# An eleventh 2 MB expert-weight buffer in place of the residual rows; one buffer each for gathered and turned token rows; silu written in the place of h

## The chip, the cores and the metric

One Trainium2 chip; the kernel runs on one core of it. Engines are named as in the profile: PE (TensorE, matmul), PEld (its weight loads), DVE (VectorE), ACT (ScalarE), POOL (GpSimd), SP (SyncE, which here only issues transfers). The metric is the device time of one execution in microseconds (us), the median of the runs shown. The kernel before: 911.71 us, median of 3 runs (910.99 to 911.99).

## What is computed

The reference is one inference step of a one-layer encoder on 512 prompt rows and 32 sample rows of width 1024, 544 rows in all. Two mixers (a state-space branch and a pooling branch) are gated, merged, projected and added to the input. The result, x2, goes through a mixture of experts, and that stage is the one which the change touches:

```python
xn = _rmsnorm(x, g).reshape(b * l, dm)
...                                   # 4 groups of 8 experts; each row picks a group, then 2 experts in it
for e in range(N_EXPERTS):            # 32
    h = jax.nn.silu(xn @ w_gate[e]) * (xn @ w_up[e])
    y = y + combine[:, e:e + 1] * (h @ w_down[e]).astype(jnp.float32)
return x + y.reshape(b, l, dm).astype(x.dtype)
```

A last rmsnorm with `g_final` follows. `w_gate[e]` and `w_up[e]` are 1024 x 512, `w_down[e]` is 512 x 1024, all float32, so each is 2 MB (2.097 million bytes), and 32 experts need 96 such loads, 201 MB.

## The kernel before, in words

Everything of the core's SBUF is one tensor, `arena`, laid out by hand with the offsets `O_...`; so nearly every operand is called `arena` in the profile. All PSUM is one tensor, `ps`. The kernel is written per engine, in program order, with semaphores; there is no scheduler.

**Up to the experts.** The two mixers take the first 312 us. The output projection then makes x2 row block by row block (`out_part`, blocks of 128 rows, `OUT_ORDER`), DVE adds the residual into `x_tok` (the residual rows, 5 blocks of 1024 words at `O_XTOK`), POOL stores x2 to DRAM (`x2_rows`, L542), and router arithmetic assigns to each expert up to 64 row slots (`TILE`). Two experts make a pair: 128 slots, 16 pairs (`NP`). When all row numbers are known (`rows_ready`), the experts begin.

**The ring.** Expert weights go to a ring of 10 buffers of 2 MB (`RING`, `NS = 10`). Load l is kind l % 3 (gate, up, down) of expert l // 3, into buffer l % NS. All loads are issued by SP, in order (L390, with L419 and L423 for the last expert, whose loads are cut in pieces). Loads 0 to 6 are issued once the mixers' areas are free, load 7 after nine of ten output halves, loads 8 and 9 after the tenth. Load l from NS on waits in `freed(l)` for the last reader of load l - NS: `gu_done` (gate and up matmuls of that expert) or `down_done` (its down matmuls).

**One expert on PE** (loop at L1667, e = 0 to 32): gate and up matmuls of expert e (`gate_up`, L1637, 32 records of 128x512), after an odd e the turn of the next pair's gathered rows (`turn_x`, L1627, 8 transposes), the down matmuls of expert e - 1 (`down`, L1652, 16), then the turn of the gate and up results of e (`turn_gate_up`, L1644, 4).

**Round about it.** POOL gathers the rows of pair j from `x2_rows` into `xg[j % 2]` (L545, an indirect transfer), at first pairs 0 and 1 at once, then each gather when the turn of the pair two before it has emptied the buffer; it also scatters each expert's result to `y_parts` (L562). DVE copies the turned rows out of PSUM, times the norm's weight, into `xg_t[j % 2]` (`x_out`, L1268). ACT copies gate and up results to `gu_rows` (L748), and after their turn writes `silu[e % 2]` (L753); DVE multiplies into `h[e % 2]` (`hidden`, L1296), which `down` reads. `result` (L1300) copies the down result to `y_sb`.

**The end.** After the last weight load SP fetches x2 back (L427, L430) into ring buffers 6 and 7; after the last scatter it fetches `y_parts` (L445); PE sums (L1712), ACT and DVE norm with `g_b` (the row `g_final`, copied to all partitions, which ACT fetched to `O_GB` before the experts), and SP stores.

Between the last expert and the sums a branch handles experts with more than 64 rows (`overflow`, `more`); it is skipped for these inputs.

## Time and profile before

| | |
|---|---|
| runs shown | 910.99, 911.71, 911.99 us (median 911.71) |
| the profiled execution: its own time | 908.8 us |
| its span (first to last instruction) | 907.2 us |
| mean granted TensorE clock | 0.95 |
| PE busy | 800.0 us (88%) |
| DVE, ACT, POOL busy | 263.9, 120.0, 128.1 us (29%, 13%, 14%) |
| moved by DMA | 251.58 MB, mean 277 GB/s |
| expert stage (first gate matmul to last down matmul) | 406.99 to 875.4 us |

The profiled execution's own time is 1.6 us over its span and 2.9 us below the median of the runs. Busy shares are averages over stages that differ: before 312 us PE is nearly always busy and the DMA engines mostly are not; in the expert stage it is the other way round. So each part of the change is to be read in the stage in which it lies. Times in the rows are us from the span's start, "idle before" is the engine's own idle time ahead of the instruction with what ended it, and the transfers' "us to landing" is from the issue to the completion.

### The profile page before, as it was taken

How to read it: one execution, taken by the hardware profiler on the slowest of the kernel's cores; microseconds unless marked ns; L12 is line 12 of the kernel's file. 1: busy time of each engine (PE TensorE's matmuls, PEld its weight loads, DVE VectorE, ACT ScalarE, POOL GpSimd, SP SyncE). 2: the span in 40 equal slices, each digit the busy share in tenths (PEclk: the TensorE clock that was granted, in tenths of full speed). 3: DMA queues.
4: the chain of work that ended last, by engine and by line, in shares of the span. 5: the costliest groups of instructions: out<-in, count | busy, mean ns of one | idle time of the engine just before them, and what ended most of it. 6: DMA issues, size and time to landing. Idle time of an engine off the chain costs nothing.

```text
span 907.2 us, 9594 instructions
## 1 busy us (share of the span) xinstructions
PE 800.0 (88%) x3838; PEld 454.2 (50%) x3839; DVE 263.9 (29%) x745; ACT 120.0 (13%) x230; POOL 128.1 (14%) x224
## 2 busy tenths in 40 slices
PE   2999999999999899949998788788789877977986
PEld 2788888878888655543333233233223323323332
DVE  3799856510011245552111111011011101110115
ACT  3210021120100042420000000000000000000012
POOL 3000004870033300010110100010010101000000
PEclk9999999999999999959999999899899889989999
DMA  9520221426200294366999999999999999999946
GB/s 305 140 94 4 90 105 29 117 93 219 74 19 1 72 424 207 116 260 219 420 428 425 427 427 426 426 428 427 428 425 426 429 426 426 425 428 429 408 170 252
DMA packets 42671, 251.58 MB, mean 277 GB/s; under 512 B 13173, under 2 KB 14025, under 8 KB 29922
## 3 DMA queue, kind: packets, MB, share of 16 engines
q1 hardware_dynamic: 35292, 236.97, 64.1%
q0 software_dynamic: 6672, 12.86, 4.1%
q10 hardware_dynamic: 662, 1.13, 0.4%
q8 instruction: 31, 0.51, 0.2%
q14 instruction: 14, 0.11, 0.0%
HBM read 245.33 MB, written 13.46 MB: 285 GB/s over the span
## 4 chain that ended last, share of the span: by engine, by line
PE 64%; DMA 31%; DVE 2%; issue 1%; ACTq 1%; ACT 0%; SPq 0%; DVEq 0%; POOLq 0%
DMA arena<-in_w_exp_up 29%; PE ps L1385 26%; PE ps L1637 14%; PE ps L1531 6%; PE ps L1652 6%; PE ps L1712 2%; PE ps L1627 1%; PE ps L1470 1%; PE ps L1465 1%; PE ps L1519 1%; PE ps L1553 1%; DVE arena L845 1%; DMA arena<-in_cache_pool 1%; PE ps L1644 1%; ACTq L604 1%
## 5 line engine op out<-in xcount | busy, mean ns | idle before, releaser
L1637 PE MATMUL ps<-arena 128*64 128x512 f32 x1024 | 253.3, 652 | 64.1 <-DMA arena<-in_w_exp_up 63.0
L1385 PE MATMUL ps<-arena 128*128 128x272 f32 x1024 | 239.0, 395 | 0.0
L1385 PEld LDWEIGHTS ps<-arena 128*128 128x128 f32 x1024 | 195.2, 191 | 40.2
L1637 PEld LDWEIGHTS ps<-arena 128*64 128x64 f32 x1024 | 85.6, 150 | 209.1 <-issue 206.6
L1652 PE MATMUL ps<-arena 128*64 128x512 f32 x512 | 116.4, 595 | 1.3 <-DVE arena L1296 1.3
L1300 DVE TENSOR_SCALAR arena<-ps,arena 128x512 f32<-128x512 f32 x32 | 24.0, 751 | 208.3 <-PE ps L1652 208.3
L798 DVE TENSOR_TENSOR arena<-arena 128x256 f32<-128x256 f32 (+10 forms) x223 | 75.5, 339 | 11.4 <-ACT arena L705 3.9
L1268 DVE TENSOR_TENSOR arena<-ps,arena 128x1024 f32<-128x1024 f32 x16 | 19.6, 1225 | 186.3 <-PE ps L1627 186.3
L1652 PEld LDWEIGHTS ps<-arena 128*64 128x64 f32 x512 | 37.5, 137 | 65.1 <-issue 61.8
L562 POOL DMA_INDIRECT y_parts<-arena x32 | 31.9, 997 | 261.9 <-DVE arena L1300 261.9
L748 ACT ACTIVATE arena<-ps,arena 128x512 f32<-128x512 f32 x32 | 22.0, 687 | 315.1 <-PE ps L1637 315.1
L1531 PE MATMUL ps<-arena 128*128 128x512 f32 x128 | 59.6, 603 | 0.0
L545 POOL DMA_INDIRECT arena<-x_rows,arena x16 | 16.6, 1036 | 179.9 <-PE ps L1627 168.0
L1531 PEld LDWEIGHTS ps<-arena 128*128 128x128 f32 x128 | 22.7, 190 | 21.7 <-issue 21.5
L1127 DVE TENSOR_TENSOR arena<-ps,arena 128x544 f32<-128x544 f32 x8 | 5.8, 724 | 88.7 <-PE ps L1385 88.7
L1644 PEld LDWEIGHTS ps<-arena 128*128 128x128 f32 x128 | 17.9, 209 | 26.9 <-issue 25.1
L648 ACT ACTIVATE arena<-ps 128x544 f32<-128x544 f32 x20 | 12.5, 625 | 135.1 <-PE ps L1385 135.1
L753 ACT ACTIVATE arena<-ps 128x256 f32<-128x256 f32 x32 | 12.3, 384 | 125.8 <-PE ps L1644 125.8
L1368 PE MATMUL ps<-arena 128*128 128x128 f32 (+1 forms) x40 | 8.9, 399 | 18.2 <-DVE arena L845 18.2
L1644 PE MATMUL ps<-arena 128*128 128x128 f32 x128 | 23.9, 310 | 0.9 <-ACT arena L748 0.9
L1712 PE MATMUL ps<-arena 128*128 128x512 f32 x48 | 22.6, 633 | 2.3 <-issue 2.3
L1627 PEld LDWEIGHTS ps<-arena 128*128 128x128 f32 x128 | 16.1, 195 | 14.9 <-issue 12.2
(222 smaller groups left out, 484.5 us busy)
## 6 DMA issues: line engine op xcount, KB each, us to landing
arena<-in_w_exp_gate SPq DMA_DIRECT2D x31, 2048.0 KB, 28.0
arena<-in_w_exp_up SPq DMA_DIRECT2D x31, 2048.0 KB, 32.2
arena<-in_w_exp_down SPq DMA_DIRECT2D x31, 2048.0 KB, 37.6
arena<-in_w_in SPq DMA_DIRECT2D x6, 2048.0 KB, 9.3
arena<-in_x_prompt SPq DMA_DIRECT2D x8, 512.0 KB, 6.4
arena<-in_w_out SPq DMA_DIRECT2D x2, 2048.0 KB, 11.0
arena<-y_parts SPq DMA_DIRECT2D x4, 1024.0 KB, 8.0
arena<-in_w_glu_a SPq DMA_DIRECT2D x1, 2048.0 KB, 10.4
```

The lines of the kernel that those rows point to most:

```text
L562: pool.indirect_dma_start(out=y_parts, out_offset=bass.IndirectOffsetOnAxis(ap=y_row[:, e:e + 1], axis=0), in_=y_sb[e % 2], in_offset=None ...
L748: act.activation(gu_rows[par], ps[:, 2 + par, :], ACT.Copy, scale=scale).then_inc(gu_copied, 1)
L798: step(dve.tensor_tensor(out_, x0, x1, op))
L1268: dve.tensor_tensor(xg_t[par][:, :, 0:t], src[:, :, 0:t], g_x.unsqueeze(2).to_broadcast((P, KD, t)), ALU.mult).then_inc(xt_ready, 1)
L1300: dve.tensor_scalar(y_sb[par], ps[:, 6 + par, :], scale, None, ALU.mult).then_inc(y_ready, 1)
L1385: last = pe.matmul(dst[:, hh, 0:HALF], w[:, k, m * P:(m + 1) * P], rhs[:, k, hh * HALF:(hh + 1) * HALF], start=(k == 0), stop=(k == kk - 1))
L1531: last = pe.matmul(ps[:, 2 * (n % 2) + half, :], m_t[:, k, i * P:(i + 1) * P], (w0, w1)[half][:, k, :], start=(k == 0), stop=(k == 7))
L1627: last = pe.transpose(*turned)
L1637: last = pe.matmul(ps[n * TILE:(n + 1) * TILE, 2 + par, :], x_t[:, k, :], w[:, k, :], start=(k == 0), stop=(k == KD - 1))
L1644: last = pe.transpose(ps[:, 4 + par, k * P:(k + 1) * P], blocks[:, k, :], ident)
L1652: last = pe.matmul(ps[half * TILE:(half + 1) * TILE, 6 + par, :], h[par][:, k, :], w_down[:, k, half * F:(half + 1) * F], start=(k == 0), ...
L1712: last = pe.matmul(ps[:, 2 * i + half, :], ident, part[:, half * F:(half + 1) * F], start=first, stop=end)
```

## The change

`NS` becomes 11: the ring gets an eleventh buffer, at `O_XTOK`, where residual row blocks 0 to 3 stood. To make room,

- the gathered rows have one buffer (`xg`, at the place of residual block 4) where they had two, and the turned rows one (`xg_t`, at `O_GB`) where they had two;
- `gu_rows` moves to `O_GC`;
- `silu` has no buffer of its own: ACT writes it into `h[par]` and DVE multiplies in place. ACT's wait before it is for `down_done` of expert e - 2 (the last reader of that `h`) in place of `h_ready`; DVE's own wait for `down_done` ahead of `hidden` goes, and so does its wait for `gu_done` ahead of `x_out`;
- since `O_GB` holds turned rows, `g_final` is fetched by SP at the end, after x2, into a ring buffer (`g_end`), where ACT fetched it ahead of the experts;
- the ring buffers that serve at the end change their numbers.

Loads 0 to 9 are issued as before. The new load 10 waits for `xg_in[0]`, the landing of the first gather (all x2 rows have been stored by then), and from load 11 on each waits for the reader of the load 11 before it.

```diff
@@ -87,7 +87,7 @@
 O_X2T = O_GC
-O_XG, O_XGT, O_GU = O_XTOK, O_XTOK + 2 * D, O_XTOK + 4 * D
-O_SILU, O_H, O_YSB = O_GC, O_GC + 512, O_GC + D
+O_XG, O_XGT, O_GU, O_YSB = O_XTOK + SLOT, O_GB, O_GC, O_GC + D
+O_H = (O_XNT + SLOT, O_SGS + SLOT)
 
 
-RING = (0, SLOT, O_D, O_F, O_SGS, O_USQ, O_UT, 2 * SLOT, O_CPOW, O_XNT)
+RING = (0, SLOT, O_D, O_F, O_SGS, O_USQ, O_UT, 2 * SLOT, O_CPOW, O_XNT, O_XTOK)
 EARLY = 7
@@ -208,11 +208,11 @@
         ring = [at(o, SLOT) for o in RING]
-        xg = [at(O_XG + n * D, D) for n in range(2)]
-        xg_t = [at(O_XGT + n * D, D).rearrange("p (k t) -> p k t", k=KD) for n in range(2)]
+        xg = at(O_XG, D)
+        xg_t = at(O_XGT, D).rearrange("p (k t) -> p k t", k=KD)
         gu_rows = [at(O_GU + n * F, F) for n in range(2)]
-        silu = [at(O_SILU + n * 4 * TILE, 4 * TILE).rearrange("p (k t) -> p k t", k=4) for n in range(2)]
-        h = [at(O_H + n * 4 * TILE, 4 * TILE).rearrange("p (k t) -> p k t", k=4) for n in range(2)]
+        h = [at(o, 4 * TILE).rearrange("p (k t) -> p k t", k=4) for o in O_H]
         y_sb = [at(O_YSB + n * F, F) for n in range(2)]
-        x2_end = [ring[6][:, i * D:(i + 1) * D] for i in range(4)] + [ring[7][:, 0:D]]
-        y_end = [ring[8 + i // 2][:, i % 2 * 2 * D:(i % 2 + 1) * 2 * D] for i in range(4)] + [ring[7][:, D:3 * D]]
-        junk2 = ring[5][:, 0:D]
+        x2_end = [ring[9][:, i * D:(i + 1) * D] for i in range(4)] + [ring[8][:, 0:D]]
+        y_end = [ring[(10, 0)[i // 2]][:, i % 2 * 2 * D:(i % 2 + 1) * 2 * D] for i in range(4)] + [ring[8][:, D:3 * D]]
+        g_end = ring[8][:, 3 * D:4 * D]
+        junk2 = ring[1][:, 0:D]
 
@@ -400,4 +400,6 @@
             sp.wait_ge(out_done, 2 * TT)
-            for l in range(EARLY + 1, NS):
+            for l in range(EARLY + 1, NS - 1):
                 load(l)
+            sp.wait_ge(xg_in[0], 16)
+            load(NS - 1)
             def freed(l):
@@ -426,6 +428,6 @@
             sp.wait_ge(down_done, NE - 3)
-            sp.dma_start(ring[6].rearrange("p (i d) -> p i d", i=4),
+            sp.dma_start(ring[9].rearrange("p (i d) -> p i d", i=4),
                          x2_rows[0:SEQ].rearrange("(i p) d -> p i d", p=P)).then_inc(x2_back, 16)
-            sp.wait_ge(gu_done, NE - 2)
             sp.dma_start(x2_end[4][0:DEC], x2_rows[SEQ:NT]).then_inc(x2_back, 16)
+            sp.dma_start(g_end, a["g_final"].rearrange("(o d) -> o d", o=1).to_broadcast((P, D))).then_inc(g_in, 16)
             sp.wait_ge(counts_ready, 1)
@@ -545,3 +547,3 @@
                 pool.indirect_dma_start(
-                    out=xg[j % 2], out_offset=None, in_=x2_rows,
+                    out=xg, out_offset=None, in_=x2_rows,
                     in_offset=bass.IndirectOffsetOnAxis(ap=x_row[:, j:j + 1], axis=0),
@@ -551,10 +553,9 @@
             pool.wait_ge(rows_ready, 1)
-            for j in range(3):
-                if j == 2:
-                    pool.wait_ge(xt_done, 1)
-                gather(j)
+            gather(0)
+            pool.wait_ge(xt_done, 1)
+            gather(1)
             for e in range(NE):
-                j = e // 2 + 3
+                j = e // 2 + 2
                 if e % 2 == 0 and j < NP:
-                    pool.wait_ge(xt_done, j - 1)
+                    pool.wait_ge(xt_done, j)
                     gather(j)
@@ -742,4 +743,2 @@
                 exps_out(n)
-            act.wait_ge(squares2, 2 * TT)
-            load(g_b, a["g_final"].rearrange("(o d) -> o d", o=1).to_broadcast((P, D)), g_in)
 
@@ -752,3 +751,3 @@
                 src = ps[:, 4 + par, :].rearrange("p (k t) -> p k t", k=4)
-                act.activation(silu[par], src[:, :, 0:TILE], ACT.Silu).then_inc(silu_ready, 1)
+                act.activation(h[par], src[:, :, 0:TILE], ACT.Silu).then_inc(silu_ready, 1)
 
@@ -760,3 +759,3 @@
                 if e >= 2:
-                    act.wait_ge(h_ready, e - 1)
+                    act.wait_ge(down_done, e - 1)
                 gate(e % 2, e + 1)
@@ -1264,6 +1263,6 @@
 
-            def x_out(par, turned, t=P):
+            def x_out(turned, t=P):
                 dve.wait_ge(xt_done, turned)
                 src = ps[:, 0:2, :].rearrange("p h (k t) -> p (h k) t", k=4)
-                dve.tensor_tensor(xg_t[par][:, :, 0:t], src[:, :, 0:t], g_x.unsqueeze(2).to_broadcast((P, KD, t)),
+                dve.tensor_tensor(xg_t[:, :, 0:t], src[:, :, 0:t], g_x.unsqueeze(2).to_broadcast((P, KD, t)),
                                   ALU.mult).then_inc(xt_ready, 1)
@@ -1271,3 +1270,3 @@
             dve.wait_ge(g_x_in, 16)
-            x_out(0, 1)
+            x_out(1)
             dve.wait_ge(count_done, 1)
@@ -1295,3 +1294,3 @@
                 src = ps[:, 4 + par, :].rearrange("p (k t) -> p k t", k=4)
-                dve.tensor_tensor(h[par], src[:, :, TILE:2 * TILE], silu[par], ALU.mult).then_inc(h_ready, 1)
+                dve.tensor_tensor(h[par], src[:, :, TILE:2 * TILE], h[par], ALU.mult).then_inc(h_ready, 1)
 
@@ -1302,10 +1301,5 @@
             for e in range(NE):
-                if e >= 2:
-                    dve.wait_ge(down_done, e - 1)
                 hidden(e % 2, e + 1)
                 if e % 2 == 0 and e + 2 < NE:
-                    j = e // 2 + 1
-                    if j >= 2:
-                        dve.wait_ge(gu_done, 2 * j - 2)
-                    x_out(j % 2, j + 1)
+                    x_out(e // 2 + 2)
                 if e >= 2:
@@ -1344,3 +1338,3 @@
                 inverse_root(mean, root_i)
-                x_i, g_i = (x.rearrange("p (h n) -> p h n", h=2) for x in (x2_end[i][:r], g_b[:r]))
+                x_i, g_i = (x.rearrange("p (h n) -> p h n", h=2) for x in (x2_end[i][:r], g_end[:r]))
                 dve.scalar_tensor_tensor(out=x_i, in0=ps[:r, 2 * i:2 * i + 2, :] if n else x_i, scalar=root_i,
@@ -1621,4 +1615,4 @@
 
-            def turn_x(par, rows):
-                blocks = xg[par].rearrange("t (q k) -> t k q", k=KD)
+            def turn_x(rows):
+                blocks = xg.rearrange("t (q k) -> t k q", k=KD)
                 for k in range(KD):
@@ -1662,3 +1656,3 @@
             pe.wait_ge(xg_in[0], 16)
-            turn_x(0, P)
+            turn_x(P)
             pe.wait_ge(rows_ready, 1)
@@ -1671,3 +1665,3 @@
                         pe.wait_ge(gu_copied, e - 1)
-                    gate_up(e % 2, xg_t[e // 2 % 2][:, :, e % 2 * TILE:(e % 2 + 1) * TILE], weights(e, 0), weights(e, 1), e + 1 == NE)
+                    gate_up(e % 2, xg_t[:, :, e % 2 * TILE:(e % 2 + 1) * TILE], weights(e, 0), weights(e, 1), e + 1 == NE)
                     if e % 2 and e + 1 < NE:
@@ -1675,3 +1669,3 @@
                         pe.wait_ge(xg_in[j % 2], 16 * (j // 2 + 1))
-                        turn_x(j % 2, P)
+                        turn_x(P)
                 if e:
```

The SP queue around the first loads that wait for a reader, before (expert loads 7 to 15; `out_done` counts halves of the output projection, `gate_up_done` and `down_done` are the semaphores `gu_done` and `down_done`):

```order
L390 DMA arena<-in_w_exp_up 128x4096 [waits out_done]
L390 DMA arena<-in_w_exp_down 128x4096 [waits out_done]
L390 DMA arena<-in_w_exp_gate 128x4096
L390 DMA arena<-in_w_exp_up 128x4096 [waits gate_up_done]
L390 DMA arena<-in_w_exp_down 128x4096 [waits gate_up_done]
L390 DMA arena<-in_w_exp_gate 128x4096 [waits down_done]
L390 DMA arena<-in_w_exp_up 128x4096 [waits gate_up_done]
L390 DMA arena<-in_w_exp_down 128x4096 [waits gate_up_done]
L390 DMA arena<-in_w_exp_gate 128x4096 [waits down_done]
```

and with the change (loads 7 to 16):

```order
L390 DMA arena<-in_w_exp_up 128x4096 [waits out_done]
L390 DMA arena<-in_w_exp_down 128x4096 [waits out_done]
L390 DMA arena<-in_w_exp_gate 128x4096
L390 DMA arena<-in_w_exp_up 128x4096 [waits xg_in0]
L390 DMA arena<-in_w_exp_down 128x4096 [waits gate_up_done]
L390 DMA arena<-in_w_exp_gate 128x4096 [waits gate_up_done]
L390 DMA arena<-in_w_exp_up 128x4096 [waits down_done]
L390 DMA arena<-in_w_exp_down 128x4096 [waits gate_up_done]
L390 DMA arena<-in_w_exp_gate 128x4096 [waits gate_up_done]
L390 DMA arena<-in_w_exp_up 128x4096 [waits down_done]
```

The up load of expert 3 (load 10) waits for the first gather and no longer for expert 0's matmuls. Behind it the pattern of waits is the same, two loads on `gate_up_done` and then one on `down_done`, with the loads moved on by one.

The POOL queue from the last x2 store, before:

```order
L542 DMA x_rows<-arena 128x1024 [waits x2_ready] x4
L545 DMA arena<-x_rows,arena 128x1024 [waits rows_ready,x2_stored]
L545 DMA arena<-x_rows,arena 128x1024
L545 DMA arena<-x_rows,arena 128x1024 [waits xg_turned] x2
L562 DMA y_parts<-arena 2176x512 [waits y_ready] x2
```

and with the change:

```order
L544 DMA x_rows<-arena 128x1024 [waits x2_ready] x4
L547 DMA arena<-x_rows,arena 128x1024 [waits rows_ready,x2_stored]
L547 DMA arena<-x_rows,arena 128x1024 [waits xg_turned] x2
L563 DMA y_parts<-arena 2176x512 [waits y_ready] x2
```

One gather stands ahead of the first turn in place of two; each later gather waits for the turn of the pair just before its own.

## Rows read from the trace of the kernel before

**Rows 1.** The page's second part: GB/s moved, 40 slices of 22.7 us each.

```profile
GB/s 305 140 94 4 90 105 29 117 93 219 74 19 1 72 424 207 116 260 219 420 428 425 427 427 426 426 428 427 428 425 426 429 426 426 425 428 429 408 170 252
```

**Rows 2.** Waits of PE, 404 to 880 us: who waited for whom, us, times, longest.

```profile
PE ps L1637 <- DMA arena<-in_w_exp_up: 63.0, 21, 5.3
```

**Rows 3.** Stretches: us, busy us of each engine, granted clock, DMA share, GB/s.

```profile
403.60:408.60 5.00, 3.84 (x14) 2.63 (x16) 2.65 (x9) 0.00 (x0) 0.99 (x1) 0.50 0.18 43
409.60:415.70 6.10, 6.10 (x28) 1.78 (x24) 2.34 (x10) 0.00 (x0) 0.00 (x0) 0.94 0.01 5
...
425.60:429.05 3.45, 3.45 (x17) 0.97 (x14) 1.09 (x1) 0.00 (x0) 0.99 (x1) 1.00 0.74 274
...
476.00:848.00 372.00, 309.04 (x1350) 121.12 (x1348) 44.08 (x62) 26.09 (x49) 34.51 (x35) 0.91 1.01 426
```

**Rows 4.** SP's queue in order of time, loads 7 to 12: start us, us.

```profile
378.44 0.33 SPq L390 DMA_DIRECT2D arena<-in_w_exp_up  x1
386.19 0.33 SPq L390 DMA_DIRECT2D arena<-in_w_exp_down  x1
386.56 0.43 SPq L390 DMA_DIRECT2D arena<-in_w_exp_gate  x1
415.76 0.33 SPq L390 DMA_DIRECT2D arena<-in_w_exp_up  x1
416.14 0.43 SPq L390 DMA_DIRECT2D arena<-in_w_exp_down  x1
429.05 0.33 SPq L390 DMA_DIRECT2D arena<-in_w_exp_gate  x1
```

**Rows 5.** PE in order of time, start of the experts: start us, us, [idle before].

```profile
403.64 1.97 PE L1627 MATMUL ps<-arena 128*128 128x128 f32 x8 [2.52 <-DMA arena<-x_rows,arena]
...
406.99 8.73 PE L1637 MATMUL ps<-arena 128*64 128x512 f32 x32 [1.12 <-DVE arena L1268]
...
424.27 1.16 PE L1627 MATMUL ps<-arena 128*128 128x128 f32 x8
...
447.77 1.16 PE L1627 MATMUL ps<-arena 128*128 128x128 f32 x8
```

**Rows 6.** POOL and ACT's queue in order of time: two gathers, and g_final's fetch.

```profile
399.30 1.09 POOL L545 DMA_INDIRECT arena<-x_rows,arena  x1 [11.59 <-DVE arena L1258]
...
426.20 0.99 POOL L545 DMA_INDIRECT arena<-x_rows,arena  x1 [18.84 <-PE ps L1627]
...
393.93 0.36 ACTq L604 DMA_DIRECT2D arena<-in_g_final  x1
```

**Rows 7.** All 16 gathers (line L545): us from issue to landing.

```profile
DMA to landing us min/median/max: 4.1/10.8/11.8
```

**Rows 8.** PE in order of time, gate and up matmuls of experts 27 to 31.

```profile
802.73 8.83 PE L1637 MATMUL ps<-arena 128*64 128x512 f32 x32 [5.12 <-DMA arena<-in_w_exp_up]
...
817.75 7.09 PE L1637 MATMUL ps<-arena 128*64 128x512 f32 x32 [0.84 <-DMA arena<-in_w_exp_up]
...
832.75 8.78 PE L1637 MATMUL ps<-arena 128*64 128x512 f32 x32 [3.80 <-DMA arena<-in_w_exp_up]
...
848.04 7.09 PE L1637 MATMUL ps<-arena 128*64 128x512 f32 x32 [1.15 <-DMA arena<-in_w_exp_up]
...
859.16 7.09 PE L1637 MATMUL ps<-arena 128*64 128x512 f32 x32
```

**Rows 9.** Costliest groups: ACT's silu, idle before it and by whom.

```profile
L753 ACT ACTIVATE arena<-ps 128x256 f32<-128x256 f32 x32 | 12.3, 384 | 125.8 <-PE ps L1644 125.8
```

**Rows 10.** SP's queue at the end: the last x2 fetch, then the results' fetch.

```profile
852.08 6.23 SPq L430 DMA_DIRECT2D arena<-x_rows  x1
880.79 2.51 SPq L445 DMA_DIRECT2D arena<-y_parts  x5
```

**Rows 11.** DMA issues, 399 to 880 us: KB each, median us to landing.

```profile
arena<-in_w_exp_up SPq DMA_DIRECT2D x28, 2048.0 KB, 32.5
...
arena<-x_rows SPq DMA_DIRECT2D x1, 128.0 KB, 22.2
```

More of the change, by code:

```diff
@@ L584, in more @@
                 pool.indirect_dma_start(
-                    out=xg[0][0:TILE], out_offset=None, in_=x2_rows,
+                    out=xg[0:TILE], out_offset=None, in_=x2_rows,
                     in_offset=bass.IndirectOffsetOnAxis(ap=ov_x_row[0:TILE], axis=0),
@@ L1322, in more @@
                 dve.tensor_scalar(ov_x_row, ov_y_row, 2, None, ALU.logical_shift_right).then_inc(ov_idx, 1)
-                x_out(0, n + NP, TILE)
+                x_out(n + NP, TILE)
                 hidden(0, n + NE)
@@ L1696, in more @@
                 pe.wait_ge(ov_x, n * 16)
-                turn_x(0, TILE)
+                turn_x(TILE)
                 pe.wait_ge(xt_ready, n + NP)
                 pe.wait_ge(ov_w, n * 48)
-                gate_up(0, xg_t[0][:, :, 0:TILE], ring[0].rearrange("p (k n) -> p k n", k=KD),
+                gate_up(0, xg_t[:, :, 0:TILE], ring[0].rearrange("p (k n) -> p k n", k=KD),
                         ring[1].rearrange("p (k n) -> p k n", k=KD))
```

## The prediction

> **What bounds the kernel now.** I first read the row of GB/s over the 40 slices of the span [rows 1]. From slice 19 on it stands at 420 to 430 until the last three slices: the expert stage moves weights at one even rate. Next the waits of PE in that stage [rows 2]: it waits 63.0 us in 21 times, all for expert weights, never over 5.3 us. Then the stretches [rows 3]: from 476 to 848 us the DMA engines are busy all the time (share 1.01) at 426 GB/s, while PE's 309.04 busy us leave 63 of 372 us. So from about 476 us on the weight stream sets the pace, PE runs a little behind it, and the end is "the landing of the last weights that PE waits for, plus PE's rest". That last wait is the one of 1.15 us before 848.04 [rows 8], for expert 30; PE then needs no more weights late.
>
> When does the stream start? SP's queue [rows 4] shows loads 8 and 9 issued at 386.19 and 386.56 us. Then SP stands until 415.76, when expert 0's gate and up matmuls are done (they began at 406.99 and last 8.73 us [rows 5]) and free two buffers. In between the engines run dry: 43 GB/s from 403.6 to 408.6 and 5 GB/s from 409.6 to 415.7 [rows 3]. That is a stretch of idle DMA time right ahead of a stage that is bound by DMA, and it exists because all ten buffers are full.
>
> **The change, part by part.**
>
> *The eleventh buffer.* Load 10 is issued when the first gather has landed. PE starts its first turn at 403.64 after waiting for just that [rows 5], so the issue comes at 403.6, 12.1 us before 415.76. How long does it occupy the engines? 2.097 MB at 426 GB/s [rows 3] are 4.92 us. A second gather (0.5 MB, 1.2 us by the same rate) runs beside it. For the start-up I take the quickest gather, 4.1 us from issue to landing [rows 7], of which 1.2 us are bytes: 2.9 us. Together 403.6 + 0.4 + 2.9 + 4.9 + 1.2 = 413.0, still before 415.76, so the load fits into the idle time entirely. From there the pattern is the old one: two loads at 415.76, then one that waits for `down_done` (at 429.05 [rows 4]) with two behind it, only each is one load further on. The small hole in the stream between 425.6 and 429.05 (274 GB/s [rows 3]), where two loads have landed and the third waits for PE, stays as it is: it depends on PE alone, which had all its weights then. So every weight from there on lands one load's time earlier: **-4.9 us**. Bounds: nothing, if the stream loses the lead again later; 4.92 us at the rate of the stage, 5.0 at the lowest rate of a full slice (420 [rows 1]). I take 4.9, since the stage shows no further slack in which it could be lost.
>
> Does the end follow? PE's waits for weights sum to 63.0 us [rows 2]; with weights 4.9 us earlier the first waits vanish and PE meets the stream again later, with about 58 us left. Before expert 29 PE waits 3.80 us and before expert 27 5.12 [rows 8], so expert 30's wait is again ended by a landing, which is 4.9 us earlier, and the 27 us of PE work behind it, like the tail of the kernel, move as a block.
>
> *One gather buffer.* Now the gather of pair j is issued after the turn of pair j - 1 and must land before its own turn. At full PE pace the turn starts at 424.27, the gather is issued at 426.20 [rows 6], 1.9 us later, and lands at most 11.8 us after that [rows 7]; the next turn is at 447.77 [rows 5]. 447.8 - 426.2 - 11.8 = 9.8 us are left. When the stream sets the pace a pair takes 30.3 us (817.75 to 848.04 [rows 8]) and 16.6 us are left. Cost 0; with the cover gone each us of a late gather would cost up to a us in each pair. On POOL what stands behind the wait for the turn is the scatter of an expert whose down matmuls follow that same turn on PE, so it isn't held up. The Trainium skill speaks against this part: "Trainium Kernel Development and Optimization", section Best Practices, tells to double-buffer so that DMA overlaps compute; by it the landing would be exposed, which is the third rival below.
>
> *The first gather alone.* It took 4.3 us (399.30 to 403.6 [rows 5, 6]) with another right behind; the quickest took 4.1 [rows 7]. A gain of 0 to 0.2 us on everything after; I take 0. That the second gather waits for the first turn costs nothing: needed at 424.27, issued near 406.
>
> *One buffer of turned rows, silu in place, fewer waits.* DVE writes the turned rows of the next pair only after their turn, which stands on PE behind the gate and up matmuls that read the old ones; so the second buffer never gave a head start. ACT's silu only ever waited for PE's turn of the results (125.8 us in 32 times [rows 9]), and that turn stands behind the down matmuls of the expert before, hence behind those that last read this `h`. The new wait is always met. Cost 0, gain 0: DVE and ACT are mostly idle here.
>
> *`g_final` late.* ACT's fetch at 393.93 [rows 6] goes: 0.5 MB, 1.2 us of engine time, but out of a stretch followed by idle time, so 0. SP issues it at the end, behind the last x2 fetch, which leaves SP at 852.08 + 6.23 = 858.3 and lands 22.2 us after its issue, at 874.3 [rows 10, 11]. The `y_parts` fetches, without which the last norm can't begin, are only issued at 880.79 [rows 10]. All of it moves 4.9 us forward together, so 1.2 us more of bytes have some 5 us of cover. Cost 0; if the cover were gone, 1.2 us.
>
> *The last expert.* Its pieces wait for the same `down_done` as before. 0.
>
> **Sum.** -4.9 us and nothing else: the profiled execution would go from 908.8 to 903.9 us. The median of the runs shown is 2.9 us higher, 911.71; the same step gives **906.8 us**.
>
> **The rivals.**
>
> 1. *The clock takes part back.* The granted clock averages 0.91 from 476 to 848 [rows 3]. After waits of 5.12 and 3.80 us gate and up matmuls take 8.83 and 8.78 us, after 0.84 and 1.15 us they take 7.09 [rows 8]. As long as PE then waits for the stream again this is covered. If the shifted meeting of PE and stream puts a slow spell behind the last wait, it isn't: +1.7 us, 908.5. For it: the pattern is bound to change early in the stage. Against: by the end it has settled, a long wait before odd experts, a short one before even, since the turn of the rows comes with the odd ones.
>
> 2. *No gain.* Somewhere the stream runs dry once more, and the lead is lost: 911.7. It needs a stretch in which the engines wait for a free buffer. Before 476 us there is the hole at 425.6; it would have to grow by 4.9 us, and loads are released there by the same matmuls as before. Later loads are issued some 30 us ahead of landing [rows 11]; nothing runs dry. If load 10 were issued late this would be the result too, but its release is the very event that starts PE.
>
> 3. *Slower: the single gather buffer binds.* Gathers run beside the weights, and with more loads waiting they could take longer. The Trainium skill ("DMA: Bandwidth & Descriptors", section Issuing engines are not separate DMA queues) says that transfers of all issuing engines run on the same 16 DMA engines and interleave; the trace agrees, with 4.1 us for the quickest gather and 10.8 for the median. The point from which it decides is 30.3 - 1.9 = 28.4 us to landing. At the 32.5 us that an up load takes [rows 11] a pair would need 34.4 us, and 15 pairs from 403.6 put the last turn at 919.6 and not at 841.5 (832.75 + 8.78 [rows 8]): some 78 us slower, 990. At 30 us it is 15 x 1.6, less the 4.9: some 931. Against it: the longest of 16 gathers took 11.8 us, with loads waiting all the time already.
>
> **How the numbers follow.** Forecast 0.80, clock 0.10, no gain 0.06, gather 0.04. A measurement of this kernel can tell about 0.2% from no change, 1.8 us. The forecast is faster by 4.9 us; the clock case by 3.2, of which I count 0.07 as faster and 0.03, where two such spells add up, as the same. So faster 0.87, same 0.09, slower 0.04. The range goes from 905.2 (5.0 for the load, 0.2 for the first gather, and the runs' own spread of half a us either way, with some rounding) to 909.6 (the clock case and another us of the runs' spread); it leaves out no gain and the gather.
>
> **What would show it.** Right: an SP issue near 403.6; GB/s of about 300 or more between 405 and 411; the release of the next two loads still at 415.8; the first wait of PE for weights one or two experts later than now; waits for weights of some 58 us; the wait before expert 30 ended by a landing near 843; the last down matmul done near 870.5; gathers landing in 12 us or less and no wait of PE for them but the first. Wrong: PE waiting for gathered rows in the stage, a second stretch of low GB/s before 850, a gate and up group of 8 us or more for expert 30 or 31, or a tail from the last down matmul to the end longer than the present 31.8 us (875.4 to 907.2).

## The result, and the profile after

| | before | the change |
|---|---|---|
| median of 9 runs each | 911.34 us (908.69 to 912.11) | 904.90 us (904.25 to 908.64) |
| the profiled execution: own time, span | 908.8, 907.2 us | 904.25, 902.7 us |
| all runs of this study: mean (number) | 911.0 us (131) | 906.4 us (28) |

The ratio is 0.9931, 95% interval 0.9916 to 0.9947: faster by 4.8 to 7.7 us. The forecast was 906.8 us and a range of 905.2 to 909.6; the median lies 0.3 us below it. Two further sets of runs of the changed kernel gave 0.9951 (0.9929 to 0.9972) and 0.9951 (0.9931 to 0.9971); over all runs the means are 4.6 us apart. One execution of e14 took 1182.54 us at a granted clock of 0.66 and is in none of these numbers; every other one is within 5 us of its kernel's median.

SP's queue in order of time, of the change, loads 7 to 13; it answers to [rows 4]:

```profile
377.35 0.33 SPq L390 DMA_DIRECT2D arena<-in_w_exp_up  x1
385.10 0.33 SPq L390 DMA_DIRECT2D arena<-in_w_exp_down  x1
385.47 0.43 SPq L390 DMA_DIRECT2D arena<-in_w_exp_gate  x1
402.26 0.33 SPq L390 DMA_DIRECT2D arena<-in_w_exp_up  x1
414.37 0.33 SPq L390 DMA_DIRECT2D arena<-in_w_exp_down  x1
414.75 0.43 SPq L390 DMA_DIRECT2D arena<-in_w_exp_gate  x1
427.66 0.33 SPq L390 DMA_DIRECT2D arena<-in_w_exp_up  x1
```

Load 10 goes out at 402.26, 12.1 us ahead of the first release. The stretches of the change (columns as in [rows 3]) show that it fits:

```profile
404.50:409.50 5.00, 3.88 (x13) 1.20 (x14) 4.52 (x16) 0.00 (x0) 1.01 (x1) 0.56 0.91 388
410.50:414.30 3.80, 3.80 (x18) 0.98 (x14) 0.41 (x3) 0.00 (x0) 0.00 (x0) 1.00 0.00 0
476.00:843.00 367.00, 306.32 (x1342) 119.26 (x1338) 42.79 (x61) 25.71 (x48) 35.48 (x35) 0.91 1.01 426
```

388 GB/s where 43 stood, then idle again (0 GB/s), then the stage at the same 426 GB/s as before. PE's waits, 400 to 880 us, and the landing of the 16 gathers (line L547 now), which answer to [rows 2] and [rows 7]:

```profile
PE ps L1631 <- DMA arena<-in_w_exp_up: 60.8, 21, 5.4
...
PE ps L1621 <- DMA arena<-x_rows,arena: 2.3, 1, 2.3
```

```profile
DMA to landing us min/median/max: 4.0/10.8/11.9
```

PE waits for gathered rows once, at the start, as before. PE in order of time, the start and experts 27 to 31 (as [rows 5] and [rows 8]):

```profile
402.29 1.97 PE L1621 MATMUL ps<-arena 128*128 128x128 f32 x8 [2.26 <-DMA arena<-x_rows,arena]
...
405.65 8.68 PE L1631 MATMUL ps<-arena 128*64 128x512 f32 x32 [1.12 <-DVE arena L1267]
...
796.59 9.47 PE L1631 MATMUL ps<-arena 128*64 128x512 f32 x32 [4.82 <-DMA arena<-in_w_exp_up]
...
811.60 7.09 PE L1631 MATMUL ps<-arena 128*64 128x512 f32 x32 [0.19 <-DMA arena<-in_w_exp_up]
...
827.89 9.18 PE L1631 MATMUL ps<-arena 128*64 128x512 f32 x32 [5.10 <-DMA arena<-in_w_exp_up]
...
843.19 7.09 PE L1631 MATMUL ps<-arena 128*64 128x512 f32 x32 [0.76 <-DMA arena<-in_w_exp_up]
...
854.32 7.09 PE L1631 MATMUL ps<-arena 128*64 128x512 f32 x32
```

Expert 30 starts at 843.19, 4.85 us earlier, just the forecast. But 1.4 us of that were won ahead of the stream (415.76 against 414.37 for the first release), so the stream itself gave only 3.5 us. To see such shares I cut each profile into three stretches: **A**, to the first release (the issue of the first load that waits for expert 0's matmuls); **B**, from there to the start of expert 30's gate and up matmuls, the last that wait for weights; **C**, from there to the end of the span. In the table "warm" stands for extra matmuls ahead of expert 0; each experiment is described below. All profiles but e6 and e7, us:

| kernel | A | expert 0's group | B | C |
|---|---|---|---|---|
| before | 415.8 | 8.73 | 432.3 | 59.2 |
| before, second (e1) | 417.8 | 10.01 | 432.2 | 61.4 |
| before, third (e12) | 419.6 | 10.08 | 432.2 | 59.4 |
| the change | 414.4 | 8.68 | 428.8 | 59.5 |
| the change, second (e5) | 417.8 | 8.51 | 428.4 | 59.1 |
| the change, third (e13) | 418.3 | 10.09 | 429.0 | 58.8 |
| load 10 held (e2) | 418.8 | 10.04 | 430.9 | 59.2 |
| before, gathers late (e3, e14) | 418.4, 417.5 | 8.51, 8.57 | 433.4, 433.3 | 59.1, 59.5 |
| before, g_final late (e4) | 418.0 | 9.95 | 432.4 | 60.8 |
| before, nine buffers (e11) | 419.1 | 9.95 | 437.0 | 59.5 |
| change, down first (e8) | 417.0 | 8.46 | 427.0 | 60.1 |
| before, warm (e9) | 412.6 | 7.09 | 432.4 | 59.3 |
| change, warm (e10) | 415.2 | 7.09 | 428.4 | 59.2 |
| change, warm and down first (e15) | 414.9 | 7.09 | 428.4 | 59.2 |

B repeats within 0.6 us for a kernel (before within 0.1); A differs by up to 4 us between profiles of one kernel. In e8 and e12 PE reached expert 30 after its weights, so B ends there with PE and not with a landing.

Where does A differ? Beside expert 0's group there is another one whose length changes: the 64 small matmuls with which the output projection begins, after PE has idled for 2.9 us. In the first two profiles of each kernel (before, e1; the change, e5):

```profile
312.26 3.66 PE L1590 MATMUL ps<-arena 128*32 128x256 f32 x64 [2.87 <-issue]
312.07 4.92 PE L1590 MATMUL ps<-arena 128*32 128x256 f32 x64 [2.87 <-issue]
311.18 3.66 PE L1584 MATMUL ps<-arena 128*32 128x256 f32 x64 [2.88 <-issue]
312.99 5.35 PE L1584 MATMUL ps<-arena 128*32 128x256 f32 x64 [2.87 <-issue]
```

It took 3.66 us in three of the 17 profiles (before, the change, e9) and 4.9 to 5.35 us in the other 14. The granted clock over the group is 1.00 in the first of these rows and 0.68 in the last. In the six profiles of the two unedited kernels the start of this group (311.2 to 313.0), its length and the length of expert 0's group account for A to within 0.5 us. So of the 1.4 us above, 1.1 were there before this group began, in code that the change doesn't touch.

### The profile page after: what moved, and what is told of

It reads as the page before. It is cut to its first block, busy times and chain, and to the rows that moved or that the text cites. A ratio compares the mean times of both kernels' runs of the same rounds, so it can differ in the third digit from the quotient of the medians.

```text
span 902.7 us, 9550 instructions
## 1 busy us (share of the span) xinstructions
PE 798.6 (88%) x3838; PEld 452.8 (50%) x3839; DVE 263.9 (29%) x745; ACT 120.0 (13%) x230; POOL 128.3 (14%) x224
## 4 chain that ended last, share of the span: by engine, by line
PE 63%; DMA 32%; DVE 2%; issue 1%; ACTq 1%; ACT 0%; SPq 0%; POOLq 0%; DVEq 0%
DMA arena<-in_w_exp_up 30%; PE ps L1379 26%; PE ps L1631 14%; PE ps L1525 6%; PE ps L1646 6%; PE ps L1706 2%; PE ps L1621 1%; PE ps L1464 1%; PE ps L1459 1%; PE ps L1513 1%; PE ps L1547 1%; DVE arena L844 1%; DMA arena<-in_cache_pool 1%; PE ps L1638 1%; DMA arena<-y_parts 1%
## 5 line engine op out<-in xcount | busy, mean ns | idle before, releaser
L1631 PE MATMUL ps<-arena 128*64 128x512 f32 x1024 | 252.0, 649 | 62.0 <-DMA arena<-in_w_exp_up 60.8
L1379 PEld LDWEIGHTS ps<-arena 128*128 128x128 f32 x1024 | 195.0, 191 | 40.1
L1646 PEld LDWEIGHTS ps<-arena 128*64 128x64 f32 x512 | 37.9, 137 | 64.4 <-issue 61.4
L547 POOL DMA_INDIRECT arena<-x_rows,arena x16 | 16.6, 1040 | 197.2 <-PE ps L1621 185.6
L1525 PEld LDWEIGHTS ps<-arena 128*128 128x128 f32 x128 | 22.8, 190 | 21.7 <-issue 21.5
L1638 PEld LDWEIGHTS ps<-arena 128*128 128x128 f32 x128 | 17.8, 208 | 26.9 <-issue 25.1
L525 POOL TENSOR_TENSOR arena<-arena 128x544 f32<-128x544 f32 x8 | 10.7, 1339 | 90.0 <-DVE arena L1126 90.0
```

What stands on the lines that cost most here:

```text
L547: pool.indirect_dma_start(out=xg, out_offset=None, in_=x2_rows, in_offset=bass.IndirectOffsetOnAxis(ap=x_row[:, j:j + 1], axis=0), bounds_ ...
L1379: last = pe.matmul(dst[:, hh, 0:HALF], w[:, k, m * P:(m + 1) * P], rhs[:, k, hh * HALF:(hh + 1) * HALF], start=(k == 0), stop=(k == kk - 1))
L1525: last = pe.matmul(ps[:, 2 * (n % 2) + half, :], m_t[:, k, i * P:(i + 1) * P], (w0, w1)[half][:, k, :], start=(k == 0), stop=(k == 7))
L1631: last = pe.matmul(ps[n * TILE:(n + 1) * TILE, 2 + par, :], x_t[:, k, :], w[:, k, :], start=(k == 0), stop=(k == KD - 1))
L1638: last = pe.transpose(ps[:, 4 + par, k * P:(k + 1) * P], blocks[:, k, :], ident)
L1646: last = pe.matmul(ps[half * TILE:(half + 1) * TILE, 6 + par, :], h[par][:, k, :], w_down[:, k, half * F:(half + 1) * F], start=(k == 0), ...
```

## The experiments

**The kernel before again (e1).** No edit.

> The kernel before, unchanged. The runs of both kernels spread over more than their step: before 908.7 to 912.1 us, the change 904.3 to 908.6. Theory A (the stream's lead alone): the spread is in the part ahead of the experts and has nothing to do with the change; this profile differs from the first one in the start of expert 0 (406.99 us there) and not behind it. Theory B (the clock): the spread comes from slow gate and up matmuls (8.8 us for 7.1) behind the last wait for weights; a profile of 911 us shows expert 30 or 31 at 8.8 us or a tail from the last landing (848.04 us there) longer than 59.2 us.

Median 912.04 us; the profile is one of 912.97. Both theories have a part, and neither has all: there is a difference behind expert 0's start. In order of time on PE, expert 0 and expert 30 of this profile:

```profile
407.72 10.01 PE L1637 MATMUL ps<-arena 128*64 128x512 f32 x32 [1.12 <-DVE arena L1268]
...
850.01 8.78 PE L1637 MATMUL ps<-arena 128*64 128x512 f32 x32 [2.85 <-DMA arena<-in_w_exp_up]
```

Of 4.2 us of span above the first profile, 2.0 are in A (1.3 each from the 64 matmuls at 312 us and from expert 0's group, 10.01 us for 8.73, less some tenths elsewhere), and 2.2 in C, 1.7 of them expert 30's group at 8.78 for 7.09: the clock rival of the prediction, seen in the kernel before. The granted clock over that group is 0.81.

**Load 10 held until the first release (e2).**

```diff
             sp.wait_ge(xg_in[0], 16)
+            sp.wait_ge(gu_done, 1)
             load(NS - 1)
```

> The change with its eleventh buffer, but load 10 held until expert 0's gate and up matmuls are done, as in the kernel before. Theory A: the gain is the one load that runs in idle time, less one gather (0.5 MB, up to 1.2 us) that now runs within the stream. Without the early issue this kernel is 4.9 us slower than the change and 0 to 1.2 us slower than before. Theory B (the clock, or g_final's and the first gather's part, give a share of the gain of 6.4 us): it is still 1 to 2.4 us faster than before.

Median 909.83 us, ratio to before 0.9984 (0.9968 to 1.0000): 1.9 us faster by the medians, where theory A said 0 to 1.2 slower. The number lies where theory B had it, but not for B's reasons: stretch C is as before, expert 0's group was slow (10.04 us), and the gain is in stretch B, 430.9 us, 1.4 shorter than before. Three loads now go out at the first release in place of two, and the third fills the hole in the stream at which [rows 3] showed 274 GB/s. The stretch from 10.5 to 15 us after the first release, before, and in this kernel:

```profile
426.26:430.76 4.50, 4.50 (x24) 1.76 (x22) 1.61 (x3) 0.38 (x1) 1.05 (x2) 1.00 0.70 199
```

```profile
429.34:433.84 4.50, 4.50 (x24) 1.71 (x22) 1.54 (x3) 0.38 (x1) 1.05 (x2) 1.00 1.04 441
```

(441 - 199) GB/s x 4.5 us are 1.1 MB, 2.6 us of stream. The change keeps the hole (231 GB/s, 424.87 to 429.37), since its eleventh load is long done by then. So in stretch B, against the kernel before with the same gathers (e3 and e14, 433.35 us), the eleventh buffer is worth 4.6 us when it is filled ahead of the experts, and 2.4 us when it is filled only with them.

**The change's gather schedule alone (e3, e14).** The kernel before, with

```diff
-            for j in range(3):
-                if j == 2:
-                    pool.wait_ge(xt_done, 1)
-                gather(j)
+            gather(0)
+            pool.wait_ge(xt_done, 1)
+            gather(1)
             for e in range(NE):
-                j = e // 2 + 3
+                j = e // 2 + 2
                 if e % 2 == 0 and j < NP:
-                    pool.wait_ge(xt_done, j - 1)
+                    pool.wait_ge(xt_done, j)
```

> The kernel before with the gathers' schedule of the change alone: gather 0 by itself, each later gather after the turn of the pair just before (the two buffers stay). Theory A: the third gather leaves the idle time before the stream and runs within it, so up to +1.2 us, less 0.2 to 0.3 us since the first gather runs alone: +0.3 to +1.0 against before, 911.6 to 912.4. Theory B: no such term, -0.3 to 0.

> The kernel before with the gathers' schedule of the change, a second profile. Theory C: 8.5 us for expert 0's group, as in its first profile, and a median 0 to 1 us above before (+1.1 in stretch B, less up to 1.4 in A). Theory D: either, and +0.9 over before on the average. Stretch B is 433.4 us by both.

Medians 912.37 (ratio 1.0019, 0.9999 to 1.0039) and 913.1 us (1.0021, 0.9996 to 1.0046). The times alone could just be no change; B is 433.4 and 433.3 us, +1.1 both times: theory A. PE never waits for a gather here but at the start. What moves is one gather. The last gather ahead of the first release is the third of before and the second of e3:

```profile
406.38 0.99 POOL L545 DMA_INDIRECT arena<-x_rows,arena  x1 [4.67 <-PE ps L1627]
```

```profile
409.23 1.01 POOL L545 DMA_INDIRECT arena<-x_rows,arena  x1 [5.66 <-PE ps L1626]
```

So 0.5 MB, 1.2 us at 426 GB/s, leave the idle time and run in the stream. With this term the change's B is 432.3 - 4.9 + 1.1 = 428.5; 428.8, 428.4 and 429.0 were measured.

**g_final at the end (e4).** The kernel before without ACT's fetch, and

```diff
             sp.dma_start(x2_end[4][0:DEC], x2_rows[SEQ:NT]).then_inc(x2_back, 16)
+            sp.dma_start(g_end, a["g_final"].rearrange("(o d) -> o d", o=1).to_broadcast((P, D))).then_inc(g_in, 16)
```

(`g_end` is free room in ring buffer 7.)

> The kernel before with g_final fetched by SP behind the last x2 fetch, and not by ACT ahead of the experts. Theory A: hidden at both places, 0 +- 0.3 us. Theory B: its 0.5 MB ahead of the first gather delayed that gather and with it the experts, so -0.5 to -1.2 us.

Median 910.99 us, ratio 0.9992 (0.9976 to 1.0008), B 432.4: no effect that the times can tell. A small one shows in the profiles, at the last expert's down matmuls, before and here:

```profile
871.71 3.65 PE L1652 MATMUL ps<-arena 128*64 128x512 f32 x16 [1.34 <-DVE arena L1296]
```

```profile
873.73 3.65 PE L1652 MATMUL ps<-arena 128*64 128x512 f32 x16 [1.06 <-DVE arena L1296]
```

This wait is 1.34 us in all eight profiles in which ACT fetches `g_final` ahead of the experts, 1.06 here and 0.99 in all eight of the changed kernel and its variants. It falls behind the last wait for weights, so some 0.3 us of it are gain. Why the fetch's place matters there, no run shows.

**The change again (e5).** No edit.

> The changed kernel once more. I read three stretches in each profile: A, to the release of the first two buffers (415.76 us in the first profile of before, 417.78 in its second); B, from there to the last landing that PE waits for, before expert 30 (432.3 and 432.2 us); C, from there to the end (59.2 and 61.4, the second with expert 30's gate and up matmuls at 8.78 us). Theory A (lead of the stream less one gather): B is 432.3 - 4.9 + 1.1 = 428.5 in every profile of the change (428.8 in its first); what the medians show beyond 3.8 us lies in A and C. Theory B: B itself varies by over 1 us between runs of one kernel, so the load is worth more in some runs.

Median 906.73 us. B 428.4, as theory A has it.

**Extra matmuls in the waits of the stage (e6, e7).** In both kernels, ahead of `gate_up`:

```diff
+                    if 8 <= e < NE - 1:
+                        for _ in range(7 if e % 2 else 4):
+                            pe.matmul(ps[:, 0, :], ident, at(O_XGT, 512), start=True, stop=True)
```

(before reads the pair's own `xg_t` there.)

> The kernel before with 7 extra matmuls (results unused) ahead of each odd expert's gate and up matmuls and 4 ahead of each even one's, experts 8 to 30, in the time in which PE waits for weights. Theory A: PE's granted clock stays at the upper level, all gate and up groups take 7.1 us, the slow spells behind the last wait (8.78 us in one profile) are gone: C = 59.2 us in the profile, 0 to 1.7 us faster than before, with a smaller spread. Rival: clock spells don't matter, or the extra matmuls delay the last experts: 0 to +2 us.

> The changed kernel with the same extra matmuls. Theory A: with the clock's share taken from both, this one is 3.8 us (0.42%) faster than the filled kernel before. Theory B (the load itself is worth 6 us): 6 us (0.67%) faster than the filled kernel before.

Medians 933.46 and 926.84 us: these fail as a test. I had sized them by the records of the last sums, and one such matmul is two records:

```profile
850.20 6.17 PE L1674 MATMUL ps<-arena 128*128 128x512 f32 x14
856.30 7.09 PE L1637 MATMUL ps<-arena 128*64 128x512 f32 x32
```

Seven take 6.17 us, more than PE waits, so from expert 8 on PE is the bound and waits for no weights. The two medians are 6.6 us apart, which looks like theory B, but is not the load's worth: the filled kernel before still waits for weights once (2.25 us, ahead of 492.24 us, with a group of 8.74 us behind it), the filled change never, and their B (454.2 and 450.2 us) differ by those two (2.25 and 1.65 us). One thing they do show: with PE always busy (500 to 860 us) the granted clock is 1.00, the upper level of 2.4 GHz, and every group takes 7.09 us. The slow groups of the other kernels are the clock's: over the two of 8.83 and 8.78 us in [rows 8] the granted clock is 0.80, so a part of each, after a wait, runs at the lower level of 1.2 GHz.

**Expert 0's down matmuls first (e8).** The change, with

```diff
             for e in range(NE + 1):
+                if e == 1:
+                    pe.wait_ge(h_ready, 1)
+                    pe.wait_ge(slot_w_ready, 1)
+                    down(0, weights(0, 2))
...
-                if e:
+                if e >= 2:
                     pe.wait_ge(h_ready, e)
...
```

> The changed kernel with expert 0's down matmuls put ahead of expert 1's gate and up matmuls, so that its down buffer is freed some 8 us earlier. The hold of load 10 showed the stream 1.4 us shorter than before and not 1.1 longer, as if a third load at the first release filled the hole in the stream near 427 (240 GB/s between 425 and 429). If so, this kernel closes that hole too: B = 426 us, 2.5 us faster than the change, about 902.4. Rival: PE, which then waits for expert 0's silu, is later with all releases up to the first wait for weights, and the gain is lost: 0 to +1 against the change.

Median 907.09 us, ratio to before 0.9958 (0.9941 to 0.9975): no gain over the change (906.8 over all runs). B is 427.0 us in this profile, 1.4 to 2.0 less than the change's and not the 426 hoped for; C is 60.1, with a wait of 2.7 us for `y_parts`. The hole is closed and another opens. Stretches 10.5 to 15 and 28 to 34 us after the first release, of this kernel:

```profile
427.50:432.00 4.50, 4.08 (x24) 2.02 (x20) 0.87 (x1) 1.07 (x2) 0.13 (x1) 1.00 1.01 433
445.00:451.00 6.00, 6.00 (x32) 2.05 (x28) 0.00 (x0) 0.26 (x1) 0.53 (x1) 1.00 0.96 366
```

and of the change:

```profile
424.87:429.37 4.50, 4.50 (x24) 1.76 (x22) 1.60 (x3) 0.38 (x1) 1.06 (x2) 1.00 0.77 231
442.37:448.37 6.00, 6.00 (x33) 2.46 (x31) 0.80 (x1) 0.69 (x1) 0.04 (x1) 1.00 0.99 418
```

Expert 1 starts 6.0 us after the first release, where it started 1.5 us after it in the change, and load 16 goes out 26.0 us after it for 24.4: the releases come later, as the rival says, and take back a part.

**Extra matmuls before expert 0 (e9, e10).** Both kernels, 10 matmuls of 128x512 in PE's waits between the last rows' logits and the first turn:

```diff
+            fill(4)
             ranks(TT - 1)
             slot_values(TT - 2)
             slot_ids(TT - 1)
+            fill(3)
             slot_values(TT - 1)
+            fill(3)
```

> The kernel before with 10 extra matmuls (results unused) in PE's waits between 389 and 404 us, while the last rows are routed and the first gather lands. In seven profiles so far expert 0's gate and up matmuls took 8.4 to 8.7 us (five times) or 9.9 to 10.0 (four times, three of them of kernels that gather as before), since the granted clock was at the lower level from about 390 us and rose at a varying point within them. Theory A: it stays at the upper level or rises earlier, the group takes 7.1 us, and the first release (stretch A) comes 1.4 to 2.9 us earlier: 1.5 to 2.5 us faster than before, with less spread. Rival: the clock falls all the same and the extra matmuls delay the routing: 0 to +1 us.

> The changed kernel with the same 10 extra matmuls. Theory A (what the change gains beyond its stretch B of -3.8 us is the luck of the clock in expert 0): 1.5 us faster than the change, and 4.0 us (0.44%) faster than the kernel before with the extra matmuls. Rival (a part of the change shortens stretch A or C by itself): 5.5 us (0.6%) faster than that one.

(The first text says seven profiles; there were ten, six at 8.43 to 8.73 and four at 9.90 to 10.04.) Medians 908.36 us, ratio 0.9979 (0.9964 to 0.9994), and 904.70 us, 0.9946 (0.9925 to 0.9968). The first group of the warm kernel before, and the granted clock from 396 to 412 us, at 1.00:

```profile
405.44 7.09 PE L1645 MATMUL ps<-arena 128*64 128x512 f32 x32 [1.24 <-DVE arena L1268]
```

```profile
396.00:412.00 16.00, 14.34 (x62) 6.31 (x62) 8.52 (x37) 0.00 (x0) 3.10 (x3) 1.00 0.45 158
```

The same stretch of e1, where the clock stays at the lower level:

```profile
396.00:412.00 16.00, 9.54 (x32) 5.86 (x34) 8.63 (x38) 1.05 (x2) 3.09 (x3) 0.50 0.54 199
```

With the clock of expert 0 taken from both, the two kernels differ by 3.7 us in the medians and 3.4 in the means: nearer to theory A (4.0) than to 5.5, though twelve and six runs with a spread of 5 us can't exclude the latter firmly. In stretch B they differ by 4.0. The spread did not shrink (905.8 to 911.1 us before), so expert 0's clock is not its main source.

**Nine buffers (e11).** The kernel before with `NS = len(RING) - 1`.

> The kernel before with nine ring buffers in place of ten; load 9 then waits for expert 0's matmuls. Theory A (each buffer is worth one load's time as long as it is filled in the idle time ahead of the experts): stretch B is 432.3 + 4.9 = 437.2 us, 4.9 us slower than before. Rival (a tenth buffer also keeps the stream from running dry later): more than 4.9, 8 us and up, with stretches of low GB/s behind 440 us.

Median 916.54 us, ratio 1.0073 (1.0054 to 1.0091). B is 437.0 us: +4.7 for one buffer less. The slope is nearly the same on both sides of ten (4.6 with the gathers' term taken out).

**Third profiles, and both edits together (e12, e13, e15).**

> The kernel before, a third profile. Open is why the medians of the two kernels differ by more (5.7 us over all runs so far) than stretch B (3.8 us). Of the profiles without extra matmuls, those with two gathers ahead of the first turn had expert 0's gate and up matmuls at 10 us in four of five (8.73 in the other), those with one gather at 8.4 to 8.7 in five of six. Theory C (the gather that runs alone shifts the start so that the clock rises earlier within the group): 10 us again here. Theory D (chance): 8.5 as likely as 10.

> The changed kernel, a third profile. Theory C: expert 0's gate and up matmuls take 8.4 to 8.7 us again. Theory D: 8.5 and 10 us are equally likely. Stretch B is 428.5 us by both.

> The changed kernel with both edits that shortened a stretch: the 10 extra matmuls ahead of expert 0, and expert 0's down matmuls ahead of expert 1. If they add: stretch A as in the other kernel with extra matmuls (expert 0's group at 7.1 us, 1.4 us or more gained), stretch B about 427 us (1.4 less than the change): 903 us. Rival: PE, slow before expert 29, eats what the stream gains, as in the profile of the second edit alone (up to 10 us for that group): 904.7, the same as with the extra matmuls alone.

Medians 910.85, 907.42 and 904.09 us. Expert 0's group took 10.08 us in e12 and 10.09 in e13, where theory C wanted 8.5 for the change. Over all profiles without extra matmuls ahead of it the group was fast in one of six with two gathers ahead of the first turn, and in six of eight with one. That leans to C, but is too few to settle, and C's own forecast for e13 failed. The change's B is 3.5 us shorter than that of before (432.2 less 428.75, three profiles each), the means are 4.6 us apart. With the 0.3 us at the last expert some 0.8 us are left; chance is enough for that (resampled from the runs, the difference of the means is 3.9 to 5.2), and theory C would fit as well. It stays open.

e15 (0.9935, 0.9911 to 0.9958) has B at 428.4, as the change: here down first adds nothing. Expert 0's down matmuls, in e8 and in e15:

```profile
419.49 3.65 PE L1646 MATMUL ps<-arena 128*64 128x512 f32 x16 [0.94 <-DVE arena L1295]
```

```profile
417.33 5.35 PE L1654 MATMUL ps<-arena 128*64 128x512 f32 x16 [0.93 <-DVE arena L1295]
```

They took 1.7 us more in e15, and load 16 went out 27.7 us after the first release, for 26.0 in e8. So what down first is worth in the stream, 1.4 us or nothing, hangs on such details. e10 and e15 lie about 2 us under the change's median over all runs (906.8), but their intervals overlap the change's.

## Why the prediction was right or wrong

- **What bounds the kernel: right.** The stream runs at 426 GB/s in both; taking one buffer away or adding one moves B by +4.7 or, with its gather term, -3.5 us.
- **The eleventh buffer, -4.9: right.** Issue at the first gather's landing, 12.1 us before the release, all of it in idle time; e3, e14 and the change leave 433.35 - 428.75 = 4.6 us for it in B. PE's first wait for weights moved from 490.26 to 499.71 us, the last down matmul was done at 870.2, and the 58 us forecast of waits was 60.8. One sign of being wrong did appear: from the last down matmul to the end it was 32.5 us, for 31.8. But e5 and e13 have 32.1 and 31.8, and e1 and e12, of the kernel before, 32.4 and 32.1: that is scatter.
- **One gather buffer, cost 0: wrong, this step was mis-sized.** It is the term of the sum that was missed. The working looked only at whether a gather lands before its turn. It does, with room, as computed, and the rival in which it doesn't never showed. But the schedule is one gather later in all, and the gather that left the idle time is in the stream: +1.1 us (e3, e14). The rule of the Trainium skill ("Trainium Kernel Development and Optimization", Best Practices), to double-buffer so that DMA overlaps compute, has the right sign here. But the trace shows no exposed wait behind it, only 1.1 us more of stream.
- **The first gather alone, silu in place, one buffer of turned rows, g_final late, the last expert: 0, right to some tenths.** The first gather landed in 4.0 us; g_final late gave some 0.3 us at the last expert (e4). Silu and the buffer of turned rows were not tried alone; B leaves no room for a cost of theirs above some tenths.
- **The hole at 425.6 stays: right**, and worth knowing: it costs 2.4 us (e2), and the working did not ask what would close it.
- **The range: wrong, and this is the step that put the measured time outside it.** The sum should have been -3.8, or -4.1 with the 0.3 at the last expert, and the median some 907.6 us. The measured one is 904.9, for a reason that is in none of the terms of the sum: **the runs' own spread, taken as half a us either way from three runs.** (Its own terms give 906.0 for the lower end, 905.5 if both kernels' spread counts; "some rounding" made it 905.2.) What the runs showed in its place: executions of the kernel before go from 907.6 to 916.3 us, and medians of 8 to 11 runs of the change are 904.9, 906.7 and 907.4.

  The executions fall into two groups. Of the 131 of before, 38 took at most 909.4 us (mean 908.5) and 93 at least 910.2 (mean 912.1). Of the 28 of the change, 11 took at most 905.8 (mean 904.8) and 17 at least 906.5 (mean 907.5), so the change is 3.7 us faster in the lower group and 4.5 in the upper. In the result's nine runs each the lower group had two of before and six of the change; in the change's two later sets it had five of 19. That is 1.9 us of luck in the change's median (904.9 for 906.8 over all its runs). The two first profiles, 908.8 and 904.25 us, are of the lower group; the four repeats (e1, e12, e5, e13) are of the upper. They differ from the first two by the 64 matmuls at 312 us (3.66 us for 4.9 to 5.35) in all four, by expert 0's group in three, and in e1 by expert 30's at 8.78 us. Late landings of `y_parts` add to it (PE waits 3.3 us for them in e4). That this is what parts the groups in the runs without a profile is likely, but not shown; nor is it known whether it matters that the sets were not all taken on one chip.
- **What was luck:** a 1.1 us error one way and some 2 us of luck the other. The forecast itself lies 0.4 us from the mean over all 28 runs, the range of 4.4 us was missed by 0.3, and neither says much of the working.
- **The clock rival** exists, but as scatter in both kernels, not as a price of the change: in all three profiles of the change expert 30 took 7.09 us.

## What to carry to other kernels

When transfers bound a stage, look for idle transfer time right ahead of it: a buffer that can be filled there is worth nearly its whole transfer (here 4.6 to 4.7 us of 4.9), one filled later only what holes it closes. By the same token count every transfer that a change moves out of idle time into the stage, even when nobody ever waits for it. And before giving a range of half a per cent, cut the profile at the points where stages meet, and repeat it: the part that a change touches may repeat within 0.6 us while the total doesn't within 4. A range taken from three runs says little when the executions fall into two groups 3 us apart.

## What the runs showed of the hardware that was not expected

- Expert 0's group takes 7.09, 8.4 to 8.7, or 9.9 to 10.1 us and nothing between, in the 17 profiles; the granted clock ahead of it (398 to 404 us) is at 0.50 in all but the three warm kernels, where ten otherwise useless matmuls bring it to 1.00 (e9, e10) or 0.74 (e15).
- After the same 2.9 us of idle time the 64 matmuls at 312 us run wholly at the upper clock in three profiles (3.66 us) and partly at the lower in 14 (4.9 to 5.35 us).
- A hole of 2.4 us in the stream, 12 us after the first release, is still there in full at expert 30, more than 400 us later (B of e2 against e3), though PE waits 62.4 and 65.6 us for weights in between.
- A 128x512 float32 matmul from `ident` is two records in the trace, 0.88 us together at the upper clock (seven in 6.17 us in e6).
